# Two pairs of matrices give their ring slots back whole: a change to the weight queue of an encoder with experts

## The reference, cut to what matters

```
def hier_moe(h, w_grp, b_grp, w_exp, b_exp, w_gate, w_up, w_down):
    ...
    for gi in range(MOE_GROUPS):
        hid = jax.nn.silu(jnp.einsum('td,edf->tef', t, w_gate[gi])) * jnp.einsum('td,edf->tef', t, w_up[gi])
        hid = hid * gate[:, gi, :, None]
        y = y + jnp.einsum('tef,efd->td', hid, w_down[gi])
```

## Time and profile before

| | us |
|---|---|
| median of 3 runs | 956.45 |
| lowest and highest of them | 955.92, 956.63 |
| the profiled execution | 958.19 |
| its span, from the first to the last instruction | 955.5 |

### The profile page before, as it was taken

How to read it: one execution, slowest core, us unless ns; L and a number is a source line. 1 busy time by engine, 2 the same in 40 slices (tenths; PEclk the granted TensorE clock), 3 DMA queues, 4 the chain that set the end, 5 groups by cost and what they waited for, 6 DMA issues and landing times.

```text
span 955.5 us, 12418 instructions
## 1 busy us (share of the span) xinstructions
PE 935.8 (98%) x4970; PEld 584.4 (61%) x4970; DVE 381.5 (40%) x792; ACT 200.4 (21%) x405; POOL 20.4 (2%) x42
## 2 busy tenths in 40 slices
PE   9999999999999999999999999999999999999996
PEld 5578745863333333387999999999576533333332
DVE  3322522352121212166665667665544511212124
ACT  3000721343122221121011011100124321212102
POOL 0110000000000000000000000000000000000000
PEclk9999999999999999999999999999999999999999
DMA  9994229469999999999786557652875899999994
GB/s 339 315 351 152 89 104 430 170 264 366 409 431 427 428 426 419 395 289 243 199 210 150 143 141 193 166 186 104 352 295 211 318 410 420 427 429 419 418 419 169
DMA packets 119750, 282.53 MB, mean 296 GB/s; under 512 B 5126, under 2 KB 83286, under 8 KB 108696
## 3 DMA queue, kind: packets, MB, share of 16 engines
q1 hardware_dynamic: 118256, 278.18, 79.1%
q0 software_dynamic: 1168, 3.40, 1.1%
q10 hardware_dynamic: 280, 0.31, 0.1%
HBM read 280.76 MB, written 1.11 MB: 295 GB/s over the span
## 4 chain that ended last, share of the span: by engine, by line
PE 91%; DMA 7%; DVE 1%; issue 0%; ACT 0%; SPq 0%; POOL 0%; DVEq 0%; POOLq 0%; ACTq 0%
PE banks L1434 84%; DMA ring<-expert_w_up_in 7%; PE banks L1437 4%; PE banks L1909 2%; DVE scratch L2817 0%; DVE h L2312 0%; DVE nrm L2449 0%; DVE nrm L2398 0%; SPq L675 0%; POOL var L1373 0%; DVE scratch L884 0%; DVE late L866 0%; ACT late L873 0%; POOLq L115 0%; DVE late L960 0%
## 5 line engine op out<-in xcount | busy, mean ns | idle before, releaser
L1434 PE MATMUL banks<-ring,scratch 128*64 128x512 f32 (+2 forms) x1696 | 421.9, 568 | 6.0 <-DMA ring<-expert_w_up_in 5.2
L1434 PEld LDWEIGHTS banks<-ring,scratch 128*64 128x64 f32 (+1 forms) x1696 | 159.5, 147 | 211.3 <-issue 210.5
L1434 PE MATMUL banks<-late,ring 128*128 128x256 f32 (+1 forms) x704 | 119.9, 330 | 0.4 <-ACT late L873 0.4
L1434 PEld LDWEIGHTS banks<-late,ring 128*128 128x128 f32 x704 | 107.5, 191 | 10.9 <-issue 1.5
L1065 ACT ACTIVATE scratch<-banks 128x512 f32<-128x512 f32 (+4 forms) x84 | 57.8, 702 | 268.8 <-PE banks L1437 180.6
L1434 PE MATMUL banks<-scratch 128*128 128x128 f32 (+5 forms) x492 | 110.5, 390 | 1.5 <-DVE scratch L2817 1.5
L2811 DVE TENSOR_SCALAR scratch<-banks 32x1024 f32<-32x1024 f32 x28 | 34.2, 1223 | 190.8 <-PE banks L1434 190.6
L1434 PEld LDWEIGHTS banks<-scratch 128*128 128x128 f32 (+2 forms) x492 | 60.8, 173 | 44.6 <-issue 38.5
L1434 PE MATMUL banks<-ring,late 128*128 128x512 f32 (+3 forms) x288 | 84.6, 442 | 0.0
L1434 PE MATMUL banks<-scratch,ring 128*128 128x128 f32 (+1 forms) x464 | 68.3, 304 | 0.0
L1434 PEld LDWEIGHTS banks<-scratch,ring 128*128 128x128 f32 x464 | 62.7, 191 | 4.9 <-DMA ring<-xkv_w_in 0.9
(11 more groups left out here) (213 smaller groups left out, 673.7 us busy)
## 6 DMA issues: line engine op xcount, KB each, us to landing
ring<-expert_w_gate_in SPq DMA_DIRECT2D x22, 2048.0 KB, 15.7
ring<-expert_w_down_in SPq DMA_DIRECT2D x18, 2048.0 KB, 14.1
ring<-odd_w_in_in SPq DMA_DIRECT2D x72, 512.0 KB, 6.6
ring<-expert_w_up_in SPq DMA_DIRECT2D x16, 2048.0 KB, 17.1
ring<-expert_w_down_in SPq DMA_DIRECT2D x40, 512.0 KB, 9.8
ring<-expert_w_up_in SPq DMA_DIRECT2D x32, 512.0 KB, 10.2
scratch<-expert_w_gate_in SPq DMA_DIRECT2D x4, 2048.0 KB, 10.0
ring<-expert_w_gate_in SPq DMA_DIRECT2D x16, 512.0 KB, 7.6
```

Source lines behind the costliest of these rows:

```text
L1434: return giving_back(nc.tensor.matmul(dst, lhsT, rhs, start=start, stop=stop))
```

## The change

`QUARTERED` loses its entries 5 and 7. The matrices 12 and 13 (`("down", 1)`) are then loaded by `load`, each as one DMA of 2 MB once its slot's old matrix (`("down", 0)`) has been read to the end, and so are 14 and 15 (`("up", 2)`) into the slots of `("up", 1)`. The three products `("gate", 0)`, `("up", 0)` and `("gate", 1)` keep their quarters. The counts of `quarter_used` and the waits that belonged to the two go. It is the same in both layers.

```
-        QUARTERED = {0: (0, 1), 2: (0,), 3: (0, 1), 5: (0, 1), 7: (0, 1)}
+        QUARTERED = {0: (0, 1), 2: (0,), 3: (0, 1)}
...
-                                sp.wait_ge((gate_ps, up_ps, gate_ps, y_ps, up_ps)[turn], l * DUOS + (1, 1, 2, 1, 2)[turn])
+                                sp.wait_ge((gate_ps, up_ps, gate_ps)[turn], l * DUOS + (1, 1, 2)[turn])
...
-                            if m in (0, 2, 4, 8) and i == 1 and c in (1, 3, 5):
+                            if m in (0, 2, 4) and i == 1 and c in (1, 3, 5):
                                 last.then_inc(quarter_used, 1)
...
-                        if q == 0 and f == 1 and i == 1 and c < QUARTERS - 1:
-                            last.then_inc(quarter_used, 1)
```

## The result

The changed kernel is slower. Its median is 961.27 us against 956.18 us for the kernel before, and the ratio is 1.0045 (95% interval 1.0032 to 1.0059). Timed again, beside 34 runs of the kernel before, the same kernel gave 1.003 (1.0014 to 1.0046). The forecast was no change, at 956.3 us, in a range up to 959.5: wrong in sign and in range.

What follows compares the result with a forecast made beforehand. TensorE was taken as busy nearly throughout, with DMA full beside it in the first expert stage. Layer 0 0.5 us later and layer 1 0.7 us earlier gave 0.2 us less, 956.45 to 956.3 us, range 954.1 to 959.5.

Steps and rivals of the forecast that it cites:

- What bounds the kernel: Whole kernel: TensorE is busy nearly throughout, and in most of the first expert stage the DMA engines are full beside it.
- a shift of the queue is passed on whole: Expert stages: later or earlier loads move TensorE's next wait equally; gains only under 2.04 us (layer 0) or 3.14 us (layer 1).
- the four waits: TensorE's waits for `expert_w_up` ahead of `("up", 2)` and `("up", 3)` in both layers: 5.2 us in all, the most to win.
- Whole loads save 0.34 us each: Expert load queue: a queued 2 MB load takes 4.9 us against 5.24 us for four quarters.
- An idle start costs 2.8 us (7.7 for 2 MB): Load queue: 2 MB issued to an idle queue lands after 7.7 us, 2.8 us more than a queued load's 4.9.
- 3 x 4.9: Both layers: the three whole loads behind the first `("down", 1)` load land 4.9 us apart, as queued loads do.
- the second rival: Restart of the load queue is slow and lasts: 1.8 to 5.2 us extra, 958.1 to 961.5 us; chance 0.18.
- Layer 1 has 2.6 us of queue left: Layer 1: the last `("gate", 2)` quarter lands 2.6 us after the new issue, leaving a hole of only 0.2 us.
- the forecast's own rule: Expert stage: product read 7.0 us, issue 0.1 us later, first load lands after 7.7 us, three more at 4.9 us each.
- layer 0's 0.5 us: Layer 0: the last `("up", 2)` load lands at 266.3 against 265.84, 0.5 us later, after a hole of 1.8 us.
- The sum: Both layers: layer 0 0.5 us later, layer 1 0.7 us earlier, 0.2 us less in all.
- The margin of the down product (1.8 us): Ahead of `("down", 1)`: its second matrix lands 1.8 us before the product starts, each layer; lateness beyond that is paid.

Runs made afterwards that it cites:

- `longer_hole`: The changed kernel with the `("down", 1)` loads held back until a quarter of `("up", 1)` was read, 1.7 us later: 965.27 us, 1.0066 to the kernel before.
- the three comparisons above: Only up matrices whole, against first and second trace of the kernel before: stretches 1.1 and 0.6 us shorter; full change against only down matrices whole: 1.8 us shorter.
- `warm_again`: Repeat of the changed kernel with two thrown-away matmuls on TensorE ahead of the wait for `("up", 2)`: 960.24 us, 1.0034 to the kernel before.
- second trace of before: The kernel before, unchanged, run and profiled once more: 957.97 us, ratio 0.9989.
- `change_again`: The changed kernel itself, timed and profiled once more: 961.74 us, 1.003 to the kernel before.

## Why the prediction was wrong, by its steps

*What bounds the kernel; a shift of the queue is passed on whole.* Right, and `longer_hole` shows it. Only the four waits bear the change, and the stretches between them account for the span of its first trace. The span of its second, 959.8 us, has 1.5 us more between the two stretches, where the clock is low from 745 to 749 us.

*Whole loads save 0.34 us each.* The size stands up as far as traces can tell: the up matrices alone are four matrices over both layers, 1.4 us by the rule, and the stretches give 0.6, 1.1 and 1.8 us by the three comparisons above. The 0.34 us is on the high side. In layer 0 of the first trace of before fifteen of the sixteen quarters land 1.28 us after the one ahead of them, 5.12 us for 2 MB or 0.22 more than a whole load, and one lands 1.69 us after it; the mean of 1.31 has that one in it. With 0.22 us the four matrices save 0.9 us.

*An idle start costs 2.8 us (7.7 for 2 MB).* Right to 0.1 us in each trace of the change.

*Then "3 x 4.9".* This step failed. The second load behind the hole takes 6.0 and 6.5 us from the first's landing, 1.1 and 1.6 us more than a queued one; the fourth lands at 267.1 and 805.2, 23.4 and 24.0 us after the first issue, where 7.7 + 14.7 = 22.4 was forecast. In the repeated change the second load of layer 0 lands only 4.9 us behind the first, but then the third lands 5.8 us behind the second, and the fourth is as late, 23.4 us after the first issue, and in layer 1 24.0; `warm_again` has 23.2 and 23.9. The restart is slow beyond its first load; why, no run here shows. That is the second rival. It put the extra loss at 5.2 us with both queues empty, and it is 1.1 + 1.6 = 2.7. I had seen its one row, 261 GB/s for 10 us, and argued it away with a 2 MB load whose slow start was inside its own 7.7 us. That load was alone; it could not show what the next one pays.

*Layer 1 has 2.6 us of queue left, "a hole of 0.2".* This failed too, but cost less: 0.8 us, against 2.7 us for the step before. The 1.6 us by which layer 1 seemed better off was an accident of one execution. The same trace could have told: the first down quarter behind, issued at 774.7, lands 8.0 us later, at 782.7, only 0.3 us after the last gate quarter and not 1.3. So 1.0 of the 2.6 us was a late landing and no work that the queue still had to do.

```profile
L675 SPq DMA_DIRECT2D ring<-expert_w_down_in x1: 328/328/328, 774.7 to 774.7; - x1
...
DMA to landing us min/median/max: 8.0/8.0/8.0
```

With 0.8 us left, as measured, the hole is 789.0 - (782.0 + 4.9) = 2.1 us. Against the second trace of before, where the last up quarter lands at 803.6 or 29.4 us after the first down product's start, the forecast's own rule gives 7.0 + 0.1 + 7.7 + 14.7 = 29.5 us: 0.1 us later, and not 0.7 us earlier. With layer 0's 0.5 us that is 0.6 us of loss; the slow restarts, 1.1 + 1.6 us, make it 3.3.

*The sum.* Forecast -0.2 us; the spans differ by +2.7, and the stretches by +2.8 against the first trace of before and by +3.3 against the second (120.9 against 117.6). From the forecast to these 3.3 us it is -0.2, 0.8 more for the margin in layer 1, and 2.7 more for the slow restarts. Against the first trace, from which the margin was read, the restarts alone are nearly the whole miss, 2.7 of 3.0 us. The ratio of 1.0030 is 2.9 us and agrees; the medians of that comparison are 4.0 us apart. The first ratio, 1.0045, is 4.3 us. Their intervals overlap, and no trace of the change shows a larger loss in the expert stages. The 1.4 us between them may well be chance: the four runs of before in the first comparison, 955.16 to 956.63 us, are as fast as those with a clock of 0.998 in the later ones (956.7 on the mean), while the four of the change have 0.991 to 0.996. The clock of those four runs of before is not on record, so this is not shown.

*The margin of the down product (1.8 us).* Used up almost exactly: in layer 1 the second down load lands at 795.5, where the product would have started, and the 48 matmuls take 10.75 us in place of 10.52. It cost nothing, as `longer_hole` shows for a case where it is overrun.

The Trainium skill ("DMA: Bandwidth & Descriptors", Anatomy of one DMA) gives, for loads issued from GpSimd, a fixed 2.0 us and bytes over 436 GB/s, an estimate of 6.8 us for a 2 MB load; each of the restarted loads of the changed kernel, issued from SyncE, took 7.7 to 7.8. The rule of the Trainium skill (same title, Rules for kernel authors) to issue early so that the fixed cost overlaps is what the change gave up. Its rule there for at least 1 MiB a transfer holds here for the rate, 428 GB/s with 2 MB and 409 with 512 KB. The fastest kernel of this study serves both: early quarters for one matrix, 2 MB loads for three.

## What to carry to other kernels

Where the DMA queue and the compute engine are both full, smaller loads that start early are an insurance against a dry queue and cost a few per cent of the rate; buy it only up to the point where the next whole load meets a queue with enough work, and take the rest whole. Here one matrix of two was enough: the whole load behind it was issued 5.3 to 5.5 us ahead of the last landing and lost nothing. Loads issued 4.1 to 5.0 us ahead mostly lost 0.4 to 1.2 us. Price a restart by the loads behind the first as well as by the first. A margin of a microsecond or two that decides a forecast's sign has to be doubted where one of two like places has it and the other has not.

## What the runs showed of the hardware

The last landing in a queue is no sign that it is still busy: in the changed kernel DMA moved 29 GB/s from 243 to 244 us, and the last load landed at 244.8.

Ahead of `("up", 2)`, a product took 8.6 to 8.8 us in place of 7.1 after pauses of 2.18, 2.23, 2.69, 2.76 (twice), 3.18, 3.19 and 3.29 us and after one of the two of 2.60 us; where the clock was looked at, it was at 1.2 GHz for some 3 us. After the other pause of 2.60 and after those of 1.84 us and less the product took 7.09 us. It can also fall where nothing was changed. In the second trace of before it is at 0.66 on the mean between 207 and 212 us, after short pauses ahead of the expert stage where the first trace had 1.00, and the stage starts 1.3 us later:

```profile
207.00:212.00 5.00, 4.31 (x25) 4.21 (x25) 2.48 (x20) 1.95 (x1) 0.00 (x0) 0.66 1.04 437
```

Seven of the fourteen traces have it at this place. In them the first down product starts at 237.9 to 238.3 us, in the other seven at 236.5 to 237.1. `change_again` has it ahead of the second expert stage instead, from 745 to 749 us. It is one source of the differences between executions of one kernel (1.7 us from the runs of before with a clock of 0.998 to those with 0.996), and about half as large as the effect that was to be measured.
